# A two-layer encoder step on one core: the first feed-forward input projection in front of the memory projections

## The chip, the core and the metric

The kernel runs on one core of a Trainium2 chip. The metric is the device time of one execution in microseconds (us). A core has TensorE (PE: matmuls, transposes), VectorE (DVE), ScalarE (ACT), GpSimd (POOL) and SyncE (SP, which here only issues DMA transfers). Each engine runs its own program in order; they meet at semaphores alone.

## What is computed

One inference step of a two-layer encoder over R = 320 rows: 256 prompt rows and 64 sample rows, width 1024. Cut to what matters here:

```
def macaron_half(x, g, w_in, w_out):
    a, b = jnp.split(rms_norm(x, g) @ w_in, 2, axis=-1)
    return x + 0.5 * ((jax.nn.silu(a) * b) @ w_out)

def memory_kv(mem, g_mem, w_mkv, g_km):
    km, vm = jnp.split(rms_norm(mem, g_mem) @ w_mkv, 2, axis=-1)
    km = rms_norm(km.reshape(B, M, H_MEM, HEAD_DIM), g_km)
    return km, vm.reshape(B, M, H_MEM, HEAD_DIM)

```

`macaron_half` (width 1024 to 2 x 2816 and back) stands before and after the attention of each layer, four times in all; `memory_kv` is computed once for each layer from the 256 memory rows. Layer 0 has differential attention beside memory attention, layer 1 forgetting attention over keys and values shared from the stream, beside memory attention. The memory's keys and values of both layers are outputs too. They are needed first in the attention of layer 0.

## The kernel before

**Precision by splits.** Every weight and every stationary or moving operand of a projection is split into a rounded part `hi` and a remainder `lo`. A product is three matmuls (whi x xhi, whi x xlo, wlo x xhi; lines 434 to 436 in `product`), eight input tiles of 128 rows make one output tile, so a tile is 24 matmuls (66 in `out`, which has 22 input tiles).

**Stages.** The table `STAGES` gives the order: mkv0, mkv1 (the memory projections, 4 tiles of 256 columns each: 2 of keys, 2 of values), in0 (44 tiles of 320 columns: 11 blocks of 2 gate and 2 up tiles), out0 (8 tiles, 4 blocks of 2), pa, attention 0, wo0, in1, out1, kv, in2, out2, pb, attention 1, wo1, in3, out3. The stage's place in the table sets the counts on which all engines wait.

**Weights.** They stream through two slots: SyncE loads 1024 KB (in `out` 704 KB) into `raw[slot]` when `lo_ready[slot]` says the last content is split; ScalarE rounds it to `whi` (`split_hi`, line 821) once TensorE is done with the old one; VectorE subtracts to `wlo` (`split_lo`, line 1109). Slot 0 holds the first two tiles of a block, slot 1 the last two.

**Inputs.** ScalarE makes xhi times the norm's gain (`input_hi`, 858), VectorE xlo (`input_lo`, 1166). The norm's scale `r` comes later: ScalarE squares the eight tiles into two buffers `sq` (`stream_square`, 864, which waits for GpSimd's sum of two squares before), GpSimd sums them (`add_squares`, 1522 and 1525), TensorE spreads the sum by one matmul after the stage's first tile (`row_norm`, 444), ScalarE takes the root after a table load (829 to 838), VectorE a Newton step (1119 to 1125). VectorE multiplies each result by `r` as it leaves its bank (kmT, vT line 1185; gate 1203; up 1207). ScalarE's silu and hhi (898, 906), VectorE's hid and hlo (1210, 1214) make the hidden tile.

**Heads.** Keys get a norm of each head: squares (854; GpSimd 1535, 1540), `head_stat` on TensorE (459, 461), `head_root` on ScalarE and VectorE, then a tail, `tail_mkv`: TensorE transposes the values (488), VectorE copies them into vm (1160), TensorE broadcasts the root through the same two banks (478), VectorE scales kmT (1142).

**The order at the start.** SyncE loads the first weight half of mkv0 and the memory in four pieces each, in turn, then slot 1, mkv1, x, in0. GpSimd issues five table loads (`const_loads`, 1594) and then sums. ScalarE splits the pieces and then squares, TensorE starts on piece 1. mkv0 has `early_split=True`: ScalarE and VectorE split mkv1's slot 0 before mkv0's norm. The input of mkv1 is prepared in mixhi, mixlo during mkv0. The tail of mkv0 lies in in0's block 0 after its tile 1, that of mkv1 after the first tile of in0's block 2, while VectorE does it right after block 1:

```
            ffn_in("in0", left_mkv, lambda j: tail_mkv(1, "mkv1") if j == 0 else None)
```

In `ffn_out`, VectorE's block is: split of slot 0, x update (1240), xlo, split of slot 1, twice.

## Time and profile before

| | us |
|---|---|
| runs, device time | 1417.89, 1419.96, 1420.51 (median 1419.96) |
| profiled execution, its own time | 1417.31 |
| its span | 1415.2 |
| TensorE busy with matmuls | 1313.8 (93%) |
| VectorE busy | 769.6 (54%) |
| ScalarE busy | 568.3 (40%) |
| GpSimd busy | 184.8 (13%) |
| mean granted clock of TensorE | 0.967 of full speed |
| first matmul of in0 / out0 / pa | 52.25 / 213.72 / 292.47 |

The times of rows count from the span's start. A row of a timeline has the start, the length, and in brackets the engine's idle time before it with what ended it. Matmuls overlap in their pipeline, so the distance between starts tells their rate, not the length. The granted clock is given as a share of 2.4 GHz; 0.50 is the lower level, 1.2 GHz.

### The profile page before, as it was taken

The page shows a single profiled execution, that of the slowest core. Times are in us where ns is not written, and L with a number is a line of the kernel's source. Part 1 is how long each engine was busy: PE and PEld are TensorE (multiplying, and loading weights), DVE is VectorE, ACT ScalarE, POOL GpSimd, SP SyncE. Part 2 cuts the span into 40 slices and gives each one's busy share as a digit, 9 for nine tenths or more (in the row PEclk, how much of TensorE's full clock was granted, in tenths as well). Part 3 has the DMA queues.
Part 4 walks back from the last instruction along what each step waited for, and adds up shares of the span by engine and source line. Part 5 has one row for each costly group of instructions (what it writes and reads, how often), then busy time and mean ns, then how long its engine had stood idle before and what let it go on. Part 6 is the DMA issues. An engine that isn't in the chain of part 4 may idle for free.

```text
span 1415.2 us, 22134 instructions
## 1 busy us (share of the span) xinstructions
PE 1313.8 (93%) x8545; PEld 1271.6 (90%) x8545; DVE 769.6 (54%) x1230; ACT 568.3 (40%) x801; POOL 184.8 (13%) x201
## 2 busy tenths in 40 slices
PE   5799999999866999999999999999995789999999
PEld 5799999998754999999999989999983569999999
DVE  5665654455764565554455565654446545656533
ACT  6543333353343453333344433333343435333331
POOL 3400000054034100000022000001061231000000
PEclk9999999999988999999999999999996999999999
DMA  7544463443220144453444434444440004444343
GB/s 247 129 149 149 148 205 135 147 175 120 91 84 1 66 162 151 150 185 124 143 163 150 145 118 148 148 142 141 164 163 35 1 27 153 149 148 148 115 159 120
DMA packets 39065, 187.38 MB, mean 132 GB/s; under 512 B 4173, under 2 KB 14163, under 8 KB 23777
## 3 DMA queue, kind: packets, MB, share of 16 engines
q1 hardware_dynamic: 37824, 183.38, 37.9%
q0 software_dynamic: 1040, 3.13, 0.9%
q8 instruction: 38, 0.62, 0.2%
q10 hardware_dynamic: 144, 0.11, 0.1%
q14 instruction: 19, 0.15, 0.0%
HBM read 179.70 MB, written 6.90 MB: 132 GB/s over the span
## 4 chain that ended last, share of the span: by engine, by line
PE 81%; DVE 7%; ACT 5%; POOL 3%; issue 3%; DMA 1%; SPq 0%; ACTq 0%; DVEq 0%; POOLq 0%
PE bank L434 24%; PE bank L436 24%; PE bank L435 24%; ACT whi L821 2%; PE bank L689 1%; PE bank L690 1%; PE bank L691 1%; POOL ew L1569 1%; DVE wlo L1109 1%; PE bank L605 1%; PE bank L623 1%; DVE qz L1149 1%; ACT ew L972 1%; DVE ew L1288 1%; POOL ssum L1525 1%
## 5 line engine op out<-in xcount | busy, mean ns | idle before, releaser
L434 PE MATMUL bank<-xhi,whi 128*128 128x320 f32 (+1 forms) x1760 | 550.7, 313 | 22.1 <-DVE xlo L1166 11.3
L435 PE MATMUL bank<-xlo,whi 128*128 128x320 f32 (+1 forms) x1760 | 547.1, 311 | 0.0
L436 PE MATMUL bank<-xhi,wlo 128*128 128x320 f32 (+1 forms) x1760 | 546.9, 311 | 0.0
L1109 DVE TENSOR_TENSOR wlo<-raw,whi 128x2048 fp32r<-128x2048 f32 (+1 forms) x183 | 378.0, 2066 | 248.0 <-ACT whi L821 248.0
L821 ACT ACTIVATE whi<-raw 128x2048 fp32r<-128x2048 f32 (+1 forms) x183 | 315.4, 1723 | 244.4 <-PE bank L436 244.3
L434 PEld LDWEIGHTS bank<-xhi,whi 128*128 128x128 f32 x1760 | 334.2, 190 | 25.3 <-issue 14.8
L435 PEld LDWEIGHTS bank<-xlo,whi 128*128 128x128 f32 x1760 | 334.5, 190 | 0.5
L436 PEld LDWEIGHTS bank<-xhi,wlo 128*128 128x128 f32 x1760 | 334.3, 190 | 0.0
L434 PE MATMUL bank<-hhi,whi 128*128 128x320 f32 x704 | 219.5, 312 | 0.3 <-DVE wlo L1109 0.2
L436 PE MATMUL bank<-hhi,wlo 128*128 128x320 f32 x704 | 217.6, 309 | 0.0
L435 PE MATMUL bank<-hlo,whi 128*128 128x320 f32 x704 | 217.5, 309 | 0.0
L434 PEld LDWEIGHTS bank<-hhi,whi 128*128 128x128 f32 x704 | 132.1, 188 | 4.1 <-DVE wlo L1109 3.8
L435 PEld LDWEIGHTS bank<-hlo,whi 128*128 128x128 f32 x704 | 132.2, 188 | 0.0
L436 PEld LDWEIGHTS bank<-hhi,wlo 128*128 128x128 f32 x704 | 132.1, 188 | 0.0
L906 ACT ACTIVATE hhi<-hid 128x320 f32 (+1 forms) x88 | 40.8, 463 | 135.1 <-DVE hid L1210 135.1
L898 ACT ACTIVATE silu<-gate 128x320 f32<-128x320 f32 x88 | 40.8, 463 | 120.4 <-DVE gate L1203 120.4
L1203 DVE TENSOR_TENSOR gate<-bank,r 128x320 f32<-128x320 f32 x88 | 42.4, 487 | 81.3 <-PE bank L436 80.8
L1522 POOL COPY ssum<-sq 128x320 f32<-128x320 f32 (+1 forms) x7 | 6.1, 877 | 557.5 <-ACT sq L939 532.4
L1525 POOL TENSOR_TENSOR ssum<-ssum,sq 128x320 f32<-128x320 f32 (+1 forms) x49 | 46.3, 945 | 227.4 <-ACT sq L939 186.8
L623 PE MATMUL bank<-early,ew 128*128 128x128 f32 x136 | 24.5, 312 | 38.6 <-POOL ew L1569 31.1
L1214 DVE TENSOR_TENSOR hlo<-hid,hhi 128x320 f32 (+1 forms) x88 | 42.9, 488 | 31.2 <-ACT hhi L906 31.2
L1207 DVE TENSOR_TENSOR up<-bank,r 128x320 f32<-128x320 f32 x88 | 42.9, 487 | 26.7 <-PE bank L436 26.7
(205 smaller groups left out, 1156.2 us busy)
## 6 DMA issues: line engine op xcount, KB each, us to landing
raw<-in_w_ffn_in SPq DMA_DIRECT2D x88, 1024.0 KB, 4.8
raw<-in_w_ffn_out SPq DMA_DIRECT2D x64, 704.0 KB, 4.1
raw<-in_w_in_a SPq DMA_DIRECT2D x10, 1024.0 KB, 4.8
raw<-in_w_out SPq DMA_DIRECT2D x8, 1024.0 KB, 4.8
raw<-in_w_kv SPq DMA_DIRECT2D x6, 1024.0 KB, 4.7
raw<-in_w_in_b SPq DMA_DIRECT2D x4, 1024.0 KB, 4.8
raw<-in_w_mkv SPq DMA_DIRECT2D x3, 1024.0 KB, 4.8
x<-in_xT SPq DMA_DIRECT2D x1, 1280.0 KB, 9.4
```

The costliest lines, as they stand in the source:

```text
L434: mm(acc, wh, mhi(ks[q]), start=start and q == 0, stop=False)
L435: mm(acc, wh, mlo(ks[q]), start=False, stop=False)
L436: last = mm(acc, wl, mhi(ks[q]), start=False, stop=stop and q == nk - 1)
L623: last = nc.tensor.transpose(aux[b][:, to:to + P], ew[:, u % 2, at:at + P], ident[:])
L821: nc.scalar.activation(whi[slot][:, 0:size], raw[slot][:, 0:size], ACT.Copy).then_inc(hi_ready[slot], 1)
L898: nc.scalar.activation(silu[:, c, :], gate[:, c, :], ACT.Silu).then_inc(silu_out, 1)
L906: nc.scalar.activation(hhi[:, bass.ds(2 * i + c, 1), :], hid[:, c:c + 1, :], ACT.Copy).then_inc(hh_ready, 1)
L1109: tt(wlo[slot][:, 0:size], raw[slot][:, 0:size], f32(whi[slot][:, 0:size]), ALU.subtract).then_inc(lo_ready[slot], 1)
L1203: tt(gate[:, c, :], banks[c][:, 0:R], r[:], ALU.mult).then_inc(acc_free, 1)
L1207: tt(up[:, c, :], banks[2 + c][:, 0:R], r[:], ALU.mult).then_inc(acc_free, 1)
L1214: tt(hlo[:, bass.ds(2 * i + c, 1), :], hid[:, c:c + 1, :], f32(hhi[:, bass.ds(2 * i + c, 1), :]), ALU.subtract).then_inc(hl_ready, 1)
L1525: nc.gpsimd.tensor_tensor(ssum[:, 0:w], ssum[:, 0:w], sq[:, k % 2, 0:w], ALU.add).then_inc(ssum_step, 1)
```

## The change

in0 becomes the first stage, mkv0 and mkv1 stand between in0 and out0. x and in0's first half come in four pieces. GpSimd issues the table loads only after the last piece has landed. The memory is loaded behind the second pair of in0; mkv0's input is prepared in two buffers of its own (memhi, memlo) by `memory_in` after in0's blocks 0 to 2. That of mkv1 is written into xhi, xlo once in0 is done with them, during mkv0. `early_split` is gone from the projections; in0 has one split ahead of its norm's silu. The tails of both layers move into out0, after its blocks 0 and 1. The stores of the memory's outputs and the cache loads stand in front of out0's last pair. The order of buffers in memory changes with it (the values go to vmT).

```diff
-STAGES = [("mkv0", 1, 4, KD), ("mkv1", 1, 4, KD),
-          ("in0", 11, 44, KD), ("out0", 8, 8, 0), ("pa", 5, 20, KD), ("wo0", 2, 8, 0),
+STAGES = [("in0", 11, 44, KD), ("mkv0", 1, 4, KD), ("mkv1", 1, 4, KD), ("out0", 8, 8, 0), ("pa", 5, 20, KD), ("wo0", 2, 8, 0),
```

SyncE:

```diff
             for q in range(4):
-                sp.dma_start(raw[0][:, 512 * q:512 * (q + 1)], a["w_mkv"][0][:, 512 * q:512 * (q + 1)]
+                sp.dma_start(x[:, 2 * q:2 * q + 2], x_v[:, 2 * q:2 * q + 2]).then_inc(d_x[q], 16)
+                sp.dma_start(raw[0][:, 512 * q:512 * (q + 1)], weights["in0"][0][:, 512 * q:512 * (q + 1)]
                              ).then_inc(d_piece[q] if q < 3 else landed[0], 16)
-                sp.dma_start(memt[:, 2 * q:2 * q + 2], mem_v[:, 2 * q:2 * q + 2]).then_inc(d_mem[q], 16)
...
+            load_stage("in0", 1, 2)
+            sp.dma_start(memt[:], a["memT"].rearrange("(k p) r -> p k r", p=P)).then_inc(d_mem, 16)
+            load_stage("in0", 2)
+            load_stage("mkv0")
             load_stage("mkv1")
...
+            load_stage("out0", 0, 7)
...
-            load_stage("out0")
...
+            load_stage("out0", 7)
```

TensorE (`biases` is the relative bias matmul after the first block's last tile):

```diff
+            def left_mkv(i):
+                if i == 0:
                     head_stat("mkv1", 0, N_MEM)
                     head_stat("mkv1", 1, N_MEM)
+                    tail_mkv(0, "mkv0")
+                else:
+                    tail_mkv(1, "mkv1")
...
-            projection("mkv1", N_MEM, [], 4, xin=(mixhi, mixlo), after=stats_mkv0)
-            ffn_in("in0", left_mkv, lambda j: tail_mkv(1, "mkv1") if j == 0 else None)
-            ffn_out("out0")
+            ffn_in("in0", biases)
+            pe.wait_ge(bias_in, 1)
+            projection("mkv0", N_MEM, [], 4, xin=(memhi, memlo))
+            projection("mkv1", N_MEM, [], 4, after=stats_mkv0)
+            ffn_out("out0", left_mkv)
```

ScalarE:

```diff
             for q in range(4):
+                act.wait_ge(d_x[q], 16)
+                for k in (2 * q, 2 * q + 1):
+                    input_hi(x[:, k, :], xhi[:, k, :], "ffn1_0", k)
                 act.wait_ge(d_piece[q] if q < 3 else landed[0], 16)
...
                 for k in (2 * q, 2 * q + 1):
-                    input_hi(memt[:, k, :], xhi[:, k, 0:N_MEM], "mem0", k)
-            for k in range(4):
-                stream_square(0, k, memt[:, k, :], N_MEM)
+                    stream_square(NORM["in0"], k, x[:, k, :], R)
             split_hi(1, 0, BLK, None, 0)
...
+            def memory_in(i):
+                if i == 0:
+                    act.wait_ge(d_mem, 16)
+                    for k in range(KD):
+                        input_hi(memt[:, k, :], memhi[:, k, :], "mem0", k)
+                else:
+                    for k in range(4 * i - 4, 4 * i):
+                        stream_square(NORM["mkv0"], k, memt[:, k, :], N_MEM)
+
+            ffn_in("in0", memory_in)
+            act.wait_ge(acc_ready, TILE0["mkv0"])
             for k in range(KD):
-                input_hi(x[:, k, :], xhi[:, k, :], "ffn1_0", k)
+                input_hi(memt[:, k, :], xhi[:, k, 0:N_MEM], "mem1", k)
```

VectorE, `ffn_out` (after each of the first two blocks, `left_mkv` does the tail of one layer), and GpSimd:

```diff
+                if after:
+                    for i in range(2):
+                        body(i, None)
+                        after(i)
...
+            pool.wait_ge(landed[0], 16)
             for dst, src in const_loads:
                 pool.dma_start(dst[:], src).then_inc(d_const, 16)
```

What it moves, at three places. **ScalarE's start**, before: `whi<-raw 128x512` is a weight piece, `xhi` two tiles of the input, `sq` their squares; the brackets name the semaphores waited for.

```order
L858 ACTIVATE xhi<-memt,early 128x256 [waits d_mem1]
L858 ACTIVATE xhi<-memt,early 128x256
L1022 ACTIVATE whi<-raw 128x512 [waits d_piece2]
L858 ACTIVATE xhi<-memt,early 128x256 [waits d_mem2]
L858 ACTIVATE xhi<-memt,early 128x256
L1022 ACTIVATE whi<-raw 128x512 [waits landed0]
L858 ACTIVATE xhi<-memt,early 128x256 [waits d_mem3]
L858 ACTIVATE xhi<-memt,early 128x256
L864 ACTIVATE sq<-memt 128x256 x2
L864 ACTIVATE sq<-memt 128x256 [waits ssum_step] x2
L821 ACTIVATE whi<-raw 128x2048 [waits landed1]
L864 ACTIVATE sq<-memt 128x256 [waits ssum_step] x4
```

Now:

```order
L1040 ACTIVATE whi<-raw 128x512 [waits d_piece1]
L879 ACTIVATE sq<-x 128x320 [waits ssum_step] x2
L873 ACTIVATE xhi<-x,early 128x320 [waits d_x2]
L873 ACTIVATE xhi<-x,early 128x320
L1040 ACTIVATE whi<-raw 128x512 [waits d_piece2]
L879 ACTIVATE sq<-x 128x320 [waits ssum_step] x2
L873 ACTIVATE xhi<-x,early 128x320 [waits d_x3]
L873 ACTIVATE xhi<-x,early 128x320
L1040 ACTIVATE whi<-raw 128x512 [waits landed0]
L879 ACTIVATE sq<-x 128x320 [waits ssum_step] x2
L836 ACTIVATE whi<-raw 128x2048 [waits landed1]
```

The squares, which wait for GpSimd's sums (`ssum_step`), moved from behind the pieces to between them. In GpSimd's program, now:

```order
L1622 DMA select<-in_select 128x1309 [waits landed0]
L1622 DMA late<-in_late 128x281
L1622 DMA hot<-in_hot 32x384
L1622 DMA table<-in_table 32x6
L1622 DMA lamv<-in_lamv 128x256
L1548 COPY ssum<-sq 128x320 [waits sq_ready]
L1551 ISA
L1551 TENSOR_TENSOR ssum<-ssum,sq 128x320 [waits ssum_step,sq_ready] x7
```

Its first table load waits for the last weight piece (`landed0`); before it waited for nothing.

**ScalarE between the two memory projections**, before (from the second layer's input on):

```order
L858 ACTIVATE mixhi<-memt,early 128x256 x8
L821 ACTIVATE whi<-raw 128x2048 [waits acc_ready,landed0]
L838 ACT_TABLE_LOAD
L829 ACTIVATE rt<-outs,early 128x256 [waits ms_ready]
L831 ACTIVATE rt<-rt 128x256 [waits root]
L833 ACTIVATE rt<-rt 128x256 [waits root]
L854 ACTIVATE hsq_hi<-kmT 128x256 [waits acc_free] x2
L821 ACTIVATE whi<-raw 128x2048 [waits acc_ready,landed1]
```

Now (from the same input on):

```order
L873 ACTIVATE xhi<-memt,early 128x256 [waits acc_ready]
L873 ACTIVATE xhi<-memt,early 128x256 x7
L853 ACT_TABLE_LOAD
L844 ACTIVATE rt<-outs,early 128x256 [waits r_ready,ms_ready]
L846 ACTIVATE rt<-rt 128x256 [waits root]
L848 ACTIVATE rt<-rt 128x256 [waits root]
L869 ACTIVATE hsq_hi<-kmT 128x256 [waits acc_free]
L836 ACTIVATE whi<-raw 128x2048 [waits acc_ready,landed0]
L869 ACTIVATE hsq_hi<-kmT 128x256 [waits acc_free]
L836 ACTIVATE whi<-raw 128x2048 [waits acc_ready,landed1]
```

The split of mkv1's slot 0 (the first `whi<-raw 128x2048`) stood before the table load and the root, and stands behind them and behind the first key tile's square (`hsq_hi`).

**The tails**, TensorE before, the one of mkv1 behind the first tile of block 2 (`early,vT` are the transposes, `rs,select` the broadcast):

```order
L436 MATMUL bank<-xhi,wlo 128x320
L488 MATMUL bank<-early,vT 128x128 [waits aux_free,acc_free,bias_in]
L488 MATMUL bank<-early,vT 128x128
L488 MATMUL bank<-early,vT 128x128 [waits aux_free]
L488 MATMUL bank<-early,vT 128x128
L478 MATMUL bank<-rs,select 128x256 [waits aux_free,hr_ready]
L478 MATMUL bank<-rs,select 128x256 [waits aux_free]
```

TensorE now, the first tail, behind out0's block 0 (`early,vmT` the transposes):

```order
L444 MATMUL bank<-hhi,wlo 128x320
L467 MATMUL outs<-hsq_hi,select 128x256 [waits hsq_ready,hr_ready]
L469 MATMUL outs<-hsq_lo,select 128x256 [waits hlo_ready]
L467 MATMUL outs<-hsq_hi,select 128x256 [waits hsq_ready]
L469 MATMUL outs<-hsq_lo,select 128x256 [waits hlo_ready]
L496 MATMUL bank<-early,vmT 128x128 [waits acc_free]
L496 MATMUL bank<-early,vmT 128x128 x3
L486 MATMUL bank<-rs,select 128x256 [waits aux_free,hr_ready]
L486 MATMUL bank<-rs,select 128x256 [waits aux_free]
L442 MATMUL bank<-hhi,whi 128x320 [waits acc_free,lo_ready0]
```

and VectorE now, from the second tile of block 0 on:

```order
L1127 TENSOR_TENSOR wlo<-raw,whi 128x1408 [waits hi_ready0]
L1257 SCALAR_TENSOR_TENSOR x<-bank,x 128x320 [waits acc_ready]
L1261 SCALAR_TENSOR_TENSOR xlo<-x,early,xhi 128x320 [waits xn_hi]
L1127 TENSOR_TENSOR wlo<-raw,whi 128x1408 [waits hi_ready1]
L1178 COPY vm<-bank 128x256 [waits aux_ready,d_scratch]
L1178 COPY vm<-bank 128x256 [waits aux_ready]
```

The broadcast waits for `aux_free`, which VectorE's copy into vm gives, behind its split of 1408 columns. Before, the tails lay in in0, with VectorE's rows for the first ahead of block 0.

## Rows read from the trace of the kernel before

**Rows 1.** The page's span; DMA view: issues, KB each, us to landing.
```profile
span 1415.2 us, 22134 instructions
...
memt<-in_memT SPq DMA_DIRECT2D x4, 256.0 KB, 7.5
...
early<-in_early ACTq DMA_DIRECT2D x1, 105.5 KB, 3.7
```

**Rows 2.** Stretches: PE, PEld, DVE, ACT, POOL busy, granted clock, DMA share, GB/s.
```profile
4.00:6.00 2.00, 0.00 (x0) 0.00 (x0) 0.00 (x0) 1.32 (x2) 0.12 (x1) 1.00 1.07 381
52.00:54.00 2.00, 1.75 (x6) 1.75 (x7) 1.79 (x4) 2.00 (x2) 1.41 (x2) 0.50 0.56 72
54.00:56.00 2.00, 2.00 (x12) 2.00 (x11) 1.90 (x6) 1.39 (x2) 0.00 (x0) 0.71 0.96 298
```

**Rows 3.** Timeline of TensorE: start us, us, line, operation [idle before <- releaser].
```profile
7.86 0.55 PE L434 MATMUL bank<-xhi,whi 128*128 128x256 f32 x1 [7.86 <-DVE xlo L1166]
...
20.09 0.39 PE L434 MATMUL bank<-xhi,whi 128*128 128x256 f32 x1 [2.13 <-DVE wlo L1109]
...
39.17 0.28 PE L434 MATMUL bank<-mixhi,whi 128*128 128x256 f32 x1
...
44.80 0.28 PE L436 MATMUL bank<-mixhi,wlo 128*128 128x256 f32 x1
...
52.25 0.64 PE L434 MATMUL bank<-xhi,whi 128*128 128x320 f32 x1 [7.17 <-DVE wlo L1109]
...
89.87 0.62 PE L478 MATMUL bank<-rs,select 64*128 64x256 f32 x2 [1.28 <-DVE vm L1160]
...
90.42 0.41 PE L434 MATMUL bank<-xhi,whi 128*128 128x320 f32 x1
...
213.72 0.31 PE L434 MATMUL bank<-hhi,whi 128*128 128x320 f32 x1
...
292.47 0.31 PE L434 MATMUL bank<-xhi,whi 128*128 128x320 f32 x1
```

**Rows 4.** Timeline of ScalarE, same columns.
```profile
5.96 0.63 ACT L1022 ACTIVATE whi<-raw 128x512 fp32r<-128x512 f32 x1
...
21.86 3.29 ACT L858 ACTIVATE mixhi<-memt,early 128x256 fp32r<-128x256 f32 x8
...
25.05 1.90 ACT L821 ACTIVATE whi<-raw 128x2048 fp32r<-128x2048 f32 x1
...
26.98 1.28 ACT L838 ACT_TABLE_LOAD   x1
...
33.83 3.72 ACT L858 ACTIVATE xhi<-x,early 128x320 fp32r<-128x320 f32 x8
...
44.71 0.47 ACT L864 ACTIVATE sq<-x 128x320 f32<-128x320 f32 x1 [0.55 <-POOL ssum L1525]
```

**Rows 5.** Timeline of VectorE, same columns.
```profile
22.39 3.74 DVE L1166 SCALAR_TENSOR_TENSOR mixlo<-memt,early,mixhi 128x256 fp32r<-128x256 f32 x8 [2.35 <-ACT mixhi L858]
...
26.99 2.29 DVE L1109 TENSOR_TENSOR wlo<-raw,whi 128x2048 fp32r<-128x2048 f32 x1 [0.86 <-ACT whi L821]
...
29.67 0.42 DVE L1119 SCALAR_TENSOR_TENSOR rt<-outs,rt 128x256 f32<-128x256 f32 x1 [0.39 <-ACT rt L833]
...
30.92 0.76 DVE L1185 TENSOR_TENSOR kmT<-bank,r 128x256 f32<-128x256 f32 x2
...
226.69 1.63 DVE L1109 TENSOR_TENSOR wlo<-raw,whi 128x1408 fp32r<-128x1408 f32 x1 [0.92 <-ACT whi L821]
```

**Rows 6.** Timeline of GpSimd, same columns; first and last of five table loads, sums.
```profile
1.24 0.74 POOL L1594 DMA_DIRECT2D select<-in_select  x1 [0.80 <-POOLq L1738]
...
3.51 0.60 POOL L1594 DMA_DIRECT2D lamv<-in_lamv  x1
...
18.08 5.38 POOL L1525 TENSOR_TENSOR ssum<-ssum,sq 128x256 f32<-128x256 f32 x4 [0.86 <-ACT sq L864]
```

**Rows 7.** Timeline of SyncE: the eighth of the nine first transfers.
```profile
5.42 0.46 SPq L368 DMA_DIRECT2D memt<-in_memT  x1
```

More of the change, by code:

```diff
@@ L209, in encoder_kernel @@
         with ExitStack() as region:
+            memhi = sb("memhi", [P, KD, N_MEM], F32R, region)
+            memlo = sb("memlo", [P, KD, N_MEM], F32R, region)
+        with ExitStack() as region:
             bias8 = sb("bias8", [P, H_A, 256], F32, region)
@@ L498, in projection @@
                     pair, slot, col = j // 4, (j // 2) % 2, j % 2
-                    if col == 0 and not (j == 0 and stage == "mkv0"):
+                    if col == 0:
                         pe.wait_ge(lo_ready[slot], n0 + pair + 1)
@@ L525, in body @@
                         slot, col = j // 2, j % 2
-                        if col == 0:
+                        if col == 0 and not (first and j == 0 and stage == "in0"):
                             pe.wait_ge(lo_ready[slot], n0 + i + 1)
@@ L531, in each @@
                             def each(k):
+                                if stage == "in0" and k % 2 == 0:
+                                    pe.wait_ge(piece_lo, k // 2 + 1) if k < 6 else pe.wait_ge(lo_ready[0], 1)
                                 pe.wait_ge(xn_lo, x0 + k + 1)
@@ L886, in projection, with ffn_in @@
                         after(j)
-            def ffn_in(stage, after_first=None, tail=None):
+            def ffn_in(stage, after=None):
                 n0, t0 = PAIR0[stage], TILE0[stage]
@@ L898, in body @@
                         nc.scalar.activation(silu[:, c, :], gate[:, c, :], ACT.Silu).then_inc(silu_out, 1)
-                        if c == 0:
+                        if c == 0 and not (stage == "in0" and isinstance(i, int) and i == 0):
                             split_hi(0, n0 + i + 1, BLK if size is None else size, acc_ready, t0 + 4 * i + 2)
@@ L1192, in projection, with ffn_in @@
                         after(j)
-            def ffn_in(stage, after_first=None, tail=None):
+            def ffn_in(stage, after=None):
                 n0, t0 = PAIR0[stage], TILE0[stage]
@@ L1198, in ffn_in @@
                     row_norm(stage, R)
+                if stage == "in0":
+                    split_lo(0, n0 + 1, BLK)
                 def body(i, size):
@@ L1203, in body @@
                         tt(gate[:, c, :], banks[c][:, 0:R], r[:], ALU.mult).then_inc(acc_free, 1)
-                    split_lo(0, n0 + i + 1, size)
+                    if not (stage == "in0" and isinstance(i, int) and i == 0):
+                        split_lo(0, n0 + i + 1, size)
                     for c in range(2):
@@ L1405, in tail_mkv @@
+            ffn_in("in0", memory_in)
+            inputs_lo("mkv1", "mem1", lambda k: memt[:, k, :], N_MEM)
+            projection("mkv0", N_MEM, 2, 4, lambda j: kmT[:, 0, j, :], lambda v: vmT[:, v, :], {})
+            projection("mkv1", N_MEM, 2, 4, lambda j: kmT[:, 1, j, :], lambda v: vmT[:, 2 + v, :], {1: "mkv0"})
             def tail_mkv(layer, st):
```

179 lines of the change are left out of this document (83 added, 96 removed).

## The prediction

> **What bounds the kernel now.** I read the page first: the span is 1415.2 us and the profiled execution itself 1417.3 [rows 1]. TensorE is the bound: in its steady part one output tile of the feed-forward input (24 matmuls of 320 columns) takes (213.72 - 90.42) / 35 = 3.52 us with nothing between [rows 3]. So a change of order can win only where TensorE now stands still or runs at its lower clock. The timeline of TensorE shows where [rows 3]. The first matmul starts at 7.86; it stands 2.13 us before 20.09 and 7.17 before 52.25, both times for VectorE's half of a weight split; a memory layer's tile takes (44.80 - 39.17 + 0.12) / 2 = 2.88 us at full clock. Everything up to the first matmul of stage pa at 292.47 is what the change rearranges; after that only one ScalarE table load in in2 goes, under TensorE work (cost nothing; if ScalarE were late there it would be 1.28 us, [rows 4]). Pure work before 292.47 is 8 x 2.88 + 44 x 3.52 + the 78.75 of out0 = 256.7 us, so 35.8 are lost there. This is what can be saved, and the question is how much the new order loses.
>
> **The clock.** After the 7.17 us pause the granted clock is 0.50 from 52 to 54 and 0.71 from 54 to 56 [rows 2]: 1.0 + 0.58 us of full speed less, minus the quarter of a microsecond before 52.25, is 1.4 us lost. I take 1.4 after each pause longer than 2 us.
>
> **1. The start.** What used to be the memory's 1024 KB is the stream's 1280 KB, in pieces between the weight pieces. ScalarE now does per piece two xhi (3.72 / 8 = 0.47 each), a 512-column split (0.63 long, the next starts after 0.55) and two squares (0.45 each), 2.4 us in all, from 5.96 on [rows 4]. Before, the squares stood behind all four pieces. Now square 2 waits for GpSimd's first sum, and GpSimd first waits for the last weight piece and issues its five table loads (1.24 to 4.11, so 2.9 us [rows 6]). The last piece's issue is the eighth, at about 5.4 [rows 7]. Landing took between 3.7 us (early) and 7.5 us (memt) [rows 1], so it lands between 9.1 and 12.9. I take 10.2, nearer the first, because GpSimd's 1 MB of tables no longer shares the way: the 2.4 MB at the 381 GB/s of 4 to 6 us [rows 2] take 6.3 us from about 2 us on. Then: tables issued 13.1, first sum 13.7, squares 2 and 3 at 13.8 and 14.7 (a square per 1.0 us at that pace, [rows 4]), piece 3's xhi and split until 16.7, two squares 17.6, piece 4 until 19.1, VectorE's half 19.7, the last squares 20.0. TensorE ends its first tile at 21.2, and the norm's matmul, which needs all eight sums (21.3), at 21.9. The next three tiles: 3 x 3.52, half of the 1.4 clock (the rest falls in the last pieces; taken as 0.5) and 0.8 for the bias matmul (an estimate, six 128 x 128 matmuls of work): the first block ends at **33.8**. Slot 1's weights are there in time: whi 20.0 to 21.9, wlo to 24.1, wanted at 26.
>
> The Trainium skill ("DMA: Bandwidth & Descriptors", Anatomy of one DMA) gives a transfer about 2.0 us fixed beside its bytes. By that, an estimate, the last piece would land at 2 + 6.3 + 2.0 = 10.3, and the sum would be 0.1 us more.
>
> **2. The other ten blocks.** 40 x 3.52 = 140.9. The memory's preparation moves into blocks 0 to 2: eight memhi on ScalarE (3.29) and eight memlo on VectorE (3.74, [rows 4, 5]). Behind them VectorE's gate products come, then ScalarE's split (1.90) and VectorE's (2.29). From block end E: hlo done E + 4.9, memlo E + 8.7, gates E + 9.7, whi E + 11.9, wlo E + 14.2, while TensorE wants it at E + 14.1. So this cover has no slack. In the next block GpSimd's squares of the memory hold ScalarE alike. I take 0.5 us; bounds 0 (it just fits) and 2 x 1.7 if a GpSimd sum is late each time. in0 ends at T = 33.8 + 140.9 + 0.5 = **175.2**.
>
> **3. mkv0 to mkv1.** TensorE: 4 x 2.88 + 0.4 for the norm = T + 11.9. Both other engines first do the second layer's input: ScalarE after its last hhi (T + 2.6) eight xhi until T + 5.9, VectorE after its split and hlo (T + 4.9) eight xlo until T + 8.7. ScalarE's table load and roots take from 26.98 to 29.67, 2.7 us [rows 4, 5], so T + 8.6; r is ready 1.25 us after VectorE starts (29.67 to 30.92), T + 10.0; first key tile 10.4, its square 10.8, whi of mkv1's slot 0 12.7, wlo T + 15.0. The early split, which stood ahead of the norm, is gone. TensorE pauses **3.1 us** and loses **1.4** of clock: mkv1 runs from T + 15.0 to 15.0 + 11.5 + 0.5 (statistics) + 1.4 = T + 28.4. Then out0's first bank waits for VectorE's third tile of mkv1, which stands behind the head root of mkv0: second tile T + 22.2, statistics, square and split until 24.4, square, table and roots 27.3, VectorE's root about 2.0 and the copy T + 29.8. Another **1.4** us. out0 starts at T + 29.8 = **205.0**, against 213.72 now: 8.7 us won so far.
>
> **4. out0.** The tails of both memory layers moved here, to the end of blocks 0 and 1. TensorE transposes the values and its next matmul, the broadcast, needs VectorE's first copy. VectorE reaches this copy only after it has finished the block. Now one such tail costs 1.28 us of waiting at 89.87 [rows 3], because TensorE does it a tile (3.5 us) after the block's end. In out0 a tile takes 78.75 / 8 = 9.84, so tile 0 ends at 213.72 + 9.84 = 223.56 and VectorE's last split, behind it, at 226.69 + 1.63 = 228.32 [rows 5]: 4.8 us later. Copy (0.4) and broadcast to stream again (90.42 - 89.87, and 0.15 to answer) make 5.9 us per block end; of these 1.2 to 1.7 are work, the rest is a pause above 4 us, with the clock's 1.4 behind it. Two of them: 2 x 7.3 = **14.6**. out0 ends at 205.0 + 78.75 + 14.6 = 298.4.
>
> **5. SP's queue.** Ahead of the last pair of out0 now stand four stores and four cache loads, 2304 KB; at 381 GB/s [rows 2] that is 6.2 us, with a 704 KB half ahead and one behind, some 10 us against a tile of 9.84 and 1.9 us of slack. Bounds 0 and 3 us, taken as 1.0, nearer zero. pa starts at **299.4**.
>
> **The sum.** 299.4 - 292.5 = +6.9 us. On the profiled execution 1417.3 that gives 1424.2; on the median of the runs shown (1420.0, which is 2.7 above it) 1426.9. I predict **1426 us**. A measurement can tell 0.2%, 2.8 us, from no change.
>
> **Rivals.** (a) *The start runs at the data's pace.* If GpSimd's sums do not hold ScalarE, piece 4 is split at 13.7 instead of 19.7: 6.0 us less, +0.9, 1421. For it: without the squares a piece costs ScalarE only 1.5 us. Against: the wait for the last piece and the five issues stand ahead of the first sum in GpSimd's program. 0.15.
> (b) *The tails in out0 cost only their work*, the other side. If VectorE had the copy done before its split, each tail would cost 1.8 us and no clock: 2 x (7.3 - 1.8) = 11.0 less, -4.1, about 1416. It decides where the pause falls under some 2.7 us per tail. For it: one tail in in0 cost a wait of 1.28 only. Against: VectorE's program has the split in front of the copy. 0.09.
> (c) *VectorE and GpSimd fall behind in blocks 0 to 2.* Four sums of GpSimd took 5.38 us from 18.08 on, beside a VectorE split, so 1.35 each and not 1.0 [rows 6]. One sum stuck behind a 2.29 us split at the start, and one in each of the two blocks, give 3 x 2.3 = 6.9, less the 0.5 taken, and with both pauses short the clock stays: +13, 1433. 0.16. The Trainium skill ("SBUF — State Buffer", SBUF: two separate sides) says that VectorE with two SBUF inputs and GpSimd take one port pair in turn, each for a whole instruction. By that rule, a sum that meets the split would wait all of it; the trace agrees in the one case above.
> (d) My forecast: 0.58; the remaining 0.02 is that the order itself has no effect.
>
> **Range and chances.** The unknowns around the forecast: landing -1.1 / +2.7, clock down to -4.7 (no fall at all), blocks -0.5 / +2.9, SP's queue -1 / +2, median or lowest run 2.7. With (a) and most of (c) inside, 1418 to 1434. Faster (below 1417.1): (b) and a tail, 0.10. Same (1417.1 to 1422.8): (a) and some of (d) by a high clock, 0.18. Slower: 0.72.
>
> **What would show it.** TensorE's first tile done at 21, a block end at 34; ScalarE's third square of the stream released by GpSimd at about 14; mkv1's first matmul released by VectorE's split after 3 us; in out0 two waits of the broadcast on VectorE's vm copy above 4 us each, with a granted clock near 0.5 behind each. I am wrong if pa starts before 292, if the waits in out0 are near 1.3, or if in0 ends much after 176.

## The result and the profile after

| | before | after |
|---|---|---|
| device time, median | 1420.24 (4 runs) | 1437.16 (1435.70 to 1439.63, 4 runs) |
| profiled execution, span | 1415.2 | 1433.9 |
| its first matmul of pa | 292.47 | 307.47 |
| from there to the span's end | 1122.7 | 1126.4 |

The ratio is 1.0123, interval [1.0103, 1.0143]: 17 us slower. The direction was forecast, the size was not: the sum had +6.9 us, the prediction was 1426 us, and the time lies 3 us above the upper end of its range (1434).

TensorE's timeline of the changed kernel, the answer to [rows 3] (start us, length us, engine, line, operation, idle time before it and what ended it):

```profile
7.71 0.60 PE L442 MATMUL bank<-xhi,whi 128*128 128x320 f32 x1 [7.71 <-DVE wlo L1398]
...
19.21 0.64 PE L442 MATMUL bank<-xhi,whi 128*128 128x320 f32 x1 [7.44 <-DVE wlo L1398]
...
24.40 0.73 PE L452 MATMUL outs<-ssum,early 128*128 128x320 f32 x1
...
36.48 0.81 PE L712 MATMUL bank<-hot,table 32*6 32x384 f32 x2
...
83.49 0.41 PE L442 MATMUL bank<-xhi,whi 128*128 128x320 f32 x1 [3.77 <-DVE wlo L1127]
...
183.69 0.28 PE L442 MATMUL bank<-memhi,whi 128*128 128x256 f32 x1
...
198.44 0.39 PE L442 MATMUL bank<-xhi,whi 128*128 128x256 f32 x1 [2.66 <-DVE wlo L1127]
...
212.15 0.38 PE L442 MATMUL bank<-hhi,whi 128*128 128x320 f32 x1 [1.47 <-issue]
...
236.68 0.62 PE L486 MATMUL bank<-rs,select 64*128 64x256 f32 x2 [4.02 <-DVE vm L1178]
...
263.60 0.82 PE L486 MATMUL bank<-rs,select 64*128 64x256 f32 x2 [4.66 <-DVE vm L1178]
...
297.70 0.41 PE L442 MATMUL bank<-hhi,whi 128*128 128x320 f32 x1 [1.97 <-DVE wlo L1127]
...
307.47 0.31 PE L442 MATMUL bank<-xhi,whi 128*128 128x320 f32 x1
```

The first block ends 0.73 us after the bias matmul starts, at 37.21. Blocks are counted from 0, so "the ten blocks" are blocks 1 to 10, and the pause before 83.49 lies before block 4. Against the forecast's marks:

| stretch | forecast | measured | difference |
|---|---|---|---|
| start to the first block's end | 33.8 | 37.21 | +3.4 |
| ten blocks | 141.4 | 146.48 | +5.1 |
| mkv0's start to out0's | 29.8 | 28.46 | -1.3 |
| out0's start to pa's | 94.4 | 95.32 | +0.9 |
| pa's start to the end | as before | +3.7 | +3.7 |

The sum of the last column, 11.8, and the forecast +6.9 make the 18.7 us between the spans.

**The start.** The timelines of ScalarE, VectorE and GpSimd, same columns:

```profile
14.31 0.47 ACT L879 ACTIVATE sq<-x 128x320 f32<-128x320 f32 x1 [5.28 <-POOL ssum L1548]
15.31 0.47 ACT L879 ACTIVATE sq<-x 128x320 f32<-128x320 f32 x1 [0.54 <-POOL ssum L1551]
...
18.85 0.61 ACT L1040 ACTIVATE whi<-raw 128x512 fp32r<-128x512 f32 x1
```

```profile
5.95 1.01 DVE L1184 SCALAR_TENSOR_TENSOR xlo<-x,early,xhi 128x320 fp32r<-128x320 f32 x2 [4.67 <-ACT xhi L873]
6.92 0.69 DVE L1398 TENSOR_TENSOR wlo<-raw,whi 128x512 fp32r<-128x512 f32 x1
...
19.08 2.23 DVE L1184 SCALAR_TENSOR_TENSOR xlo<-x,early,xhi 128x320 fp32r<-128x320 f32 x2
21.24 1.35 DVE L1398 TENSOR_TENSOR wlo<-raw,whi 128x512 fp32r<-128x512 f32 x1
```

```profile
10.93 0.74 POOL L1622 DMA_DIRECT2D select<-in_select  x1 [10.49 <-DMA raw<-in_w_ffn_in]
...
14.43 7.60 POOL L1551 TENSOR_TENSOR ssum<-ssum,sq 128x320 f32<-128x320 f32 x7 [0.16 <-POOL ssum L1548]
```

GpSimd waits for the last piece (landed at 10.6; 10.2 was taken), issues five loads, and only then makes its first sum; ScalarE's third square stands 5.28 us for it. So far this is the forecast (13.8 for that square). But VectorE's pair of xlo takes 2.23 us beside GpSimd's sums where it took 1.01 without them, and the piece's split 1.35 instead of 0.69. The last piece is done at 22.6, not at 19.7.

**Block 4.** ScalarE waits for a block of weights, and TensorE for VectorE's half behind it. The stretches (PE, PEld, DVE, ACT, POOL busy, granted clock, DMA share, GB/s) and the DMA view of the changed kernel from 50 to 85 us and, behind it, of the kernel before from 35 to 60 us (issues, KB each, us to landing):

```profile
79.12 1.91 ACT L836 ACTIVATE whi<-raw 128x2048 fp32r<-128x2048 f32 x1 [6.13 <-DMA raw<-in_w_ffn_in]
```

```profile
76.00:78.00 2.00, 2.00 (x16) 2.00 (x15) 0.00 (x0) 0.00 (x0) 0.00 (x0) 1.00 0.24 102
...
84.00:86.00 2.00, 2.00 (x11) 2.00 (x10) 1.25 (x3) 1.49 (x2) 0.00 (x0) 0.57 0.70 184
```

```profile
bias_scratch<-trel POOLq DMA_DIRECT2D x1, 576.0 KB, 18.8
```

```profile
raw<-in_w_ffn_in SPq DMA_DIRECT2D x3, 1024.0 KB, 9.6
...
bias_scratch<-trel POOLq DMA_DIRECT2D x1, 576.0 KB, 19.3
```

GpSimd writes the table of relative positions (6 partitions, short rows) to DRAM. The write is issued at 57.05 and has landed at 75.9. The 1024 KB issued at 64.35 land 14.7 us later, at 79.0, while 4.8 is the median. In the stretch from 76 to 78 us the write is done, and what is left of the loads still keeps only 0.24 of the DMA engines' time busy. Before, the same write was issued at 37.91 and took 19.3 us. Only one block of weights was issued while it ran (at 52.38, landing in 9.6 us), and TensorE has no pause behind it: there it was hidden.

**out0.** VectorE at the first tail: the split of slot 1 stands in front of the copy, as forecast.

```profile
234.57 1.63 DVE L1127 TENSOR_TENSOR wlo<-raw,whi 128x1408 fp32r<-128x1408 f32 x1 [1.07 <-ACT whi L836]
236.12 0.75 DVE L1178 COPY vm<-bank 128x256 f32<-128x256 f32 x2
```

Near its end SyncE issues four stores from 281.52, then four cache loads, then at 287.36 the last pair's weights, while the DMA engines are full:

```profile
281.52 0.40 SPq L366 DMA_DIRECT2D o_mkT<-kmT  x1
...
287.36 3.58 SPq L351 DMA_DIRECT2D raw<-in_w_ffn_out  x2
```

```profile
290.00:292.00 2.00, 2.00 (x15) 1.91 (x14) 0.57 (x1) 0.00 (x0) 0.00 (x0) 1.00 1.08 408
```

### The profile page after: what moved, and what is told of

It reads as the page before. It is cut to its first block, busy times and chain, and to the rows that moved or that the text cites. A ratio compares the mean times of both kernels' runs of the same rounds, so it can differ in the third digit from the quotient of the medians.

```text
span 1433.9 us, 22025 instructions
## 1 busy us (share of the span) xinstructions
PE 1320.0 (92%) x8545; PEld 1276.9 (89%) x8545; DVE 771.5 (54%) x1230; ACT 565.5 (39%) x799; POOL 182.9 (13%) x201
## 4 chain that ended last, share of the span: by engine, by line
PE 78%; DVE 7%; issue 5%; ACT 4%; POOL 3%; DMA 2%; SPq 1%; ACTq 0%; POOLq 0%; DVEq 0%
PE bank L442 23%; PE bank L444 23%; PE bank L443 23%; ACT whi L836 2%; DVE wlo L1127 2%; DMA raw<-in_w_ffn_in 1%; PE bank L701 1%; PE bank L703 1%; PE bank L702 1%; POOL ew L1595 1%; PE bank L617 1%; PE bank L635 1%; DVE qz L1167 1%; ACT ew L987 1%; PE bank L486 1%
## 5 line engine op out<-in xcount | busy, mean ns | idle before, releaser
L635 PEld LDWEIGHTS bank<-early,ew 128*128 128x128 f32 x136 | 17.3, 156 | 44.3 <-POOL ew L1595 35.3
L1228 DVE TENSOR_TENSOR up<-bank,r 128x320 f32<-128x320 f32 x88 | 42.9, 488 | 24.5 <-PE bank L444 24.4
```

Of the source, the lines that this page charges most:

```text
L635: last = nc.tensor.transpose(aux[b][:, to:to + P], ew[:, u % 2, at:at + P], ident[:])
L1228: tt(up[:, c, :], banks[2 + c][:, 0:R], r[:], ALU.mult).then_inc(acc_free, 1)
```

## Experiments

All start from the changed kernel. Times are medians, beside before's on the same chip. The last five columns are read from the profiled execution: "pa" is where TensorE starts on it, "behind pa" the time from there to the span's end; none means under 1 us.

| kernel | time, us | ratio, interval | first block's end | out0 starts | wait before the last pair | pa | behind pa |
|---|---|---|---|---|---|---|---|
| changed | 1437.16 | 1.0123 [1.0103, 1.0143] | 37.21 | 212.15 | 1.97 | 307.47 | 1126.4 |
| tables at once | 1433.07 | 1.0092 [1.0075, 1.0109] | 33.45 | 208.90 | 3.44 | 307.79 | 1123.4 |
| squares behind | 1435.17 | 1.0111 [1.0094, 1.0128] | 35.45 | 211.05 | 2.58 | 309.04 | 1124.2 |
| start alone | 1439.19 | 1.0145 [1.0117, 1.0172] | 38.03 | 213.53 | 1.99 | 310.91 | 1124.8 |
| table in paced pieces | 1431.56 | 1.0080 [1.0057, 1.0102] | 38.91 | 208.29 | 2.82 | 306.02 | 1124.1 |
| table whole, late | 1439.87 | 1.0138 [1.0123, 1.0154] | 37.29 | 215.01 | 1.86 | 310.82 | 1123.1 |
| pieces at once | 1435.35 | 1.0114 [1.0097, 1.0131] | 37.34 | 211.78 | 1.65 | 307.54 | 1123.4 |
| tails later | 1426.51 | 1.0049 [1.0032, 1.0065] | 38.08 | 213.40 | 2.98 | 300.79 | 1124.3 |
| early split back | 1434.21 | 1.0097 [1.0074, 1.0120] | 37.19 | 209.85 | 2.37 | 307.24 | 1126.5 |
| loads before stores | 1429.52 | 1.0066 [1.0043, 1.0089] | 37.57 | 212.72 | none | 305.78 | 1121.8 |
| all, order of "start alone" | 1413.64 | 0.9958 [0.9945, 0.9971] | 39.10 | 206.55 | none | 289.20 | 1124.8 |
| all, squares between | 1408.93 | 0.9921 [0.9908, 0.9935] | 32.91 | 200.35 | none | 282.98 | 1122.6 |

The intervals of "tables at once", "squares behind", "early split back", "pieces at once", "table whole, late" and "start alone" overlap with that of the changed kernel: what these edits are worth in the whole time is not settled, and they are read by their marks in the profile. The marks vary too. Six kernels besides the changed one share its program up to the table's write, and their first block ends between 37.19 and 38.91 with the changed kernel's at 37.21; a difference under 2 us there says little.

### The start

```diff
-            pool.wait_ge(landed[0], 16)
             for dst, src in const_loads:
```

> GpSimd issues its five table loads at once, as in the kernel before, with nothing else changed. Theory A (GpSimd's wait for the last piece plus 2.9 us of issues holds ScalarE's third square, which stood until 14.3): that square starts at about 8.5, the last piece is split at about 14 to 15 and not 22.6, the first block of in0 ends at about 32 and not 37.2; 4 to 5 us less than the change, ratio to before about 1.009. Rival B (the start is bound by the data, and the tables now share the way): the last pieces land near 12 to 13 and the first block ends at 35 or later, 0 to 2 us less.

Without GpSimd's wait the first block ends 3.8 us earlier, clear of that spread: the wait held the start. The loads do share the way, as rival B has it: the last piece lands at 12.9 instead of 10.6, so the wait had bought 2.3 us there. VectorE stays slow beside the sums (2.23 and 1.35 us), so the last piece is done at 18.0 and not at theory A's 14 to 15. The time is 4.1 us less, theory A's 4 to 5, but not for its reason: in the profile nothing of the gain is left where pa starts (307.79 against 307.47), and the 3.0 us that the span is shorter behind it belong to the open point at the end of the next section.

The next kernel leaves GpSimd's wait and puts the squares behind the four pieces:

> ScalarE's eight squares stand behind the four pieces, as in the kernel before; GpSimd's wait stays. Theory A (the squares between the pieces hold them, and GpSimd's sums slow VectorE's piece operations): the last piece is split before 15 with VectorE's xlo pairs at 1.0 us and the 512-column subtraction at 0.7 (they took 2.2 and 1.35 beside the sums), but the norm's matmul still waits for the eighth sum at about 22, so the first block ends at about 34.5, 2 to 3 us less than the change. Rival B (the sums, not the pieces, set the whole start, and slot 1's split behind the squares comes late): the first block ends at 36 to 37, no gain.

VectorE is now as fast as alone (1.01 and 0.68 us per piece), which shows what had slowed it, and the last piece is done at 12.5. TensorE then stands 7.88 us for the last sum and does the norm's matmul at 21.62 instead of 24.40. Behind this pause its matmuls start at the slow distance for longer (13.8 us from there to the block's end, 12.8 in the changed kernel), so 1.8 us are left at the block's end, between the two theories and about the size of the spread named above.

The third takes both, with slot 1's split in the middle of the squares:

```diff
-                for k in (2 * q, 2 * q + 1):
-                    stream_square(NORM["in0"], k, x[:, k, :], R)
+            for k in range(4):
+                stream_square(NORM["in0"], k, x[:, k, :], R)
             split_hi(1, 0, BLK, None, 0)
+            for k in range(4, KD):
+                stream_square(NORM["in0"], k, x[:, k, :], R)
```

> Only the start differs from the changed kernel: GpSimd's table loads issued at once, and the second slot's split after the first four squares instead of after all eight. Theory A (the start's 3.4 us over the forecast are GpSimd's wait for the last piece, which holds up the squares, and with them the norm and the split of slot 1): the first block with the bias product ends at 32.5 to 33.5 instead of 37.21, the time is 4 us less, 1433. Theory B (VectorE slowed beside GpSimd's sums is what costs, and both orders run them side by side): the first block ends at 34.5 or later, 1435 or more.

Theory A missed: the block ends at 38.03, no earlier than in the changed kernel. Theory B's numbers hold, but it is not VectorE that is slowed (1.01 and 0.69 us at every piece). TensorE, and GpSimd's sums by line (count, then length min/median/max in ns):

```profile
24.27 1.43 PE L452 MATMUL outs<-ssum,early 128*128 128x320 f32 x2 [8.54 <-POOL ssum L1553]
```

```profile
L1553 POOL TENSOR_TENSOR ssum<-ssum,sq x7: 857/861/2608, 15.0 to 23.4; 128x320 f32<-128x320 f32 x7
```

The sums begin only at 14.2, behind the four pieces, and one took 2608 ns instead of 861: the one that began at 18.6 beside VectorE's 2048-column split (18.20 to 20.49). So the norm's matmul comes at 24.27, where it was at 24.40. That is what the prediction's rival (c) had named, found at the start and not in the blocks.

### The table of relative positions

Eight pieces of 72 KB, one block of in0 apart:

```diff
-            pool.dma_start(scratch.rearrange("p h x -> h p x"),
-                           trel[:].unsqueeze(1).broadcast_to([H_A, 64, NREL + 1])).then_inc(d_scratch, 16)
...
+            for q in range(8):
+                pool.wait_ge(acc_ready, 4 * (q + 3))
+                pool.dma_start(scratch.rearrange("p h x -> h p x")[:, 8 * q:8 * q + 8],
+                               trel[:].unsqueeze(1).broadcast_to([H_A, 8, NREL + 1])).then_inc(d_scratch, 16)
```

> The one 576 KB transfer of the bias table into its scratch is cut into eight of 72 KB, each issued by GpSimd one block of in0 apart, from block 2 on. Theory A (this transfer held the weight load issued at 64.35, which took 14.7 us instead of 4.8, and so TensorE for 3.8 us before 83.49 and some 1.3 of clock): no weight load in in0 takes over 8 us, no wait before block 4, in0 ends about 5 us earlier (178 to 179), ratio about 1.0085. Rival B (the load was late through SyncE's queue or the memory's 1 MB in front of it, whatever the scratch transfer does): the load stays near 14 us and the wait near 3.8.

No wait is left in the ten blocks, and no load there takes over 5.2 us; the blocks take 140.9 us, which is 40 tiles of 3.52: theory A. Then the whole transfer, but 65 us later:

> Only the write of the table of relative positions is moved: whole as in the changed kernel (one transfer of 576 KB), but started when the seventh block of the first projection is done (about 122 us) instead of at 57. Theory A (any 1 MB block of weights issued while that transfer runs lands some 10 us late, wherever it stands, and the buffers cover only part of that): the wait of 3.8 us before block 4 at 83.5 is gone, and one of 2 to 5 us stands between 135 and 160, ScalarE's wait for raw ahead of it; the time stays at 1436 to 1438. Theory B (only the crowd of early transfers, with the memory's own load and the first blocks catching up, made the wait): no wait over 1 us anywhere in the eleven blocks, and the time is 1432, as with the eight pieces.

Its timelines of TensorE and ScalarE have the wait where theory A put it:

```profile
147.46 0.63 PE L442 MATMUL bank<-xhi,whi 128*128 128x320 f32 x1 [4.30 <-DVE wlo L1127]
```

```profile
143.10 1.91 ACT L836 ACTIVATE whi<-raw 128x2048 fp32r<-128x2048 f32 x1 [8.11 <-DMA raw<-in_w_ffn_in]
```

The block of weights issued at 126.49 took 16.5 us, the write beside it 18.2. So it is the transfer, not the crowd at the start; the time itself came out 2 us above theory A's. And the eight pieces without pauses between them:

> The write of the table of relative positions is issued where the change has it (57 us), but as eight transfers of 72 KB one after the other, without a pause between them. The bytes and their time are the same, only the cut is another. Theory A (the whole transfer has only a few DMA engines, since the 0.24 to 0.32 of the engines' time at 74 to 80 us is nearly all its own; eight small ones are dealt out over more engines): all eight have landed within 12 us of the first issue instead of 18.8, the blocks of weights of that time land within 8 us, and the wait before block 4 falls under 1 us: 1432. Theory B (it is the 576 KB of short rows that cost, however they are cut): the last piece lands some 19 us after the first issue, the wait before block 4 stays at 3 to 4.5 us, and the time at 1436 to 1438.

Theory B for the transfers. The DMA engines' time is nearly full, at 33 GB/s where the share is 0.76 (stretches of this kernel, columns as above), and the last piece lands 14.7 us after its issue at 61.2: the whole takes 18.7 us, as in one transfer. Theory A leaned on shares of 0.24 to 0.32 at 74 to 80 us in the changed kernel as the write's own; but the write had landed at 75.9, and from 76 on they are the loads'. The wait before block 4 fell to 0.69 us, but the loads were not freed: the block of weights is issued at 68.16 instead of 64.35 and lands at 78.7, against 79.0 in the changed kernel.

```profile
60.00:64.00 4.00, 4.00 (x30) 4.00 (x29) 0.00 (x0) 1.35 (x4) 3.63 (x7) 1.00 1.06 95
64.00:68.00 4.00, 1.76 (x13) 1.50 (x11) 2.31 (x2) 2.01 (x2) 0.74 (x1) 1.00 0.76 33
```

TensorE comes to it later because of a pause that neither theory had: 2.36 us before 68.12. ScalarE's and GpSimd's timelines give its chain: the eight issues stand ahead of the memory's first sum in GpSimd's program, and ScalarE's square, and the silu and the split behind it, wait for that sum.

```profile
62.18 0.42 ACT L879 ACTIVATE sq<-memt 128x256 f32<-128x256 f32 x1 [7.52 <-POOL ssum L1548]
```

```profile
57.18 4.57 POOL L1626 DMA_DIRECT2D bias_scratch<-trel  x8 [35.24 <-DVE trel L1410]
```

Block 4 starts at 83.15 instead of 83.49. The ten blocks take 144.5 us, between 140.9 and 146.5; most of the 2.0 us won is the clock, which reads 0.57 behind block 4's pause in the changed kernel and 1.00 here. Of these three ways only the paced pieces, behind the sums, cost nothing.

### The tails in out0

TensorE gets each tail half a tile later, between the two halves of the next block's first tile:

```diff
-                    after(0)
-                    body(1, False)
-                    after(1)
+                    body(1, False, lambda: after(0))
+                    body(2, False, lambda: after(1))
```

> TensorE does the two tails in out0 half a tile later (behind the first 33 matmuls of the next block) and VectorE's program stays. Theory A (TensorE stood 4.0 and 4.7 us for VectorE's copy behind its split, and then ran at the lower clock): each wait falls under 1 us, no clock loss behind it, out0 is 9 to 11 us shorter (95.3 now), ratio about 1.005. Rival B (the copy itself or the answer between the engines is slow, or ScalarE's head root for mkv1 holds VectorE): the waits move along with the tails and stay above 3 us.

The largest single gain, 10.7 us, and theory A, though out0 became 7.9 us shorter and not 9 to 11. Its two tails on TensorE wait 0.46 and 0.39 us instead of 4.02 and 4.66, and out0 takes 87.4 us instead of 95.3. The rest went at the last pair: its pause grew from 1.97 to 2.98 us, and from there to pa TensorE took 11.3 us instead of 9.8, at the lower clock. Of the 10.7 us, 2.1 lie behind pa, where the program is unchanged.

### Between mkv0 and mkv1, and the queue

> The change dropped the rule that, in mkv0, the split of slot 0 for the next stage goes ahead of the squares and the leaving of the tiles. This kernel puts the rule back on ScalarE and VectorE; nothing else differs from the changed kernel. Theory A (the pause between mkv0 and mkv1, 2.66 us ended by VectorE's weight split, is caused by the order on the two engines): the pause falls under 1 us, the clock of the tiles behind it comes back (1.4), out0 starts at 208 to 209.5 instead of 212.15, the whole is 3 to 4 us less, about 1433.5. Theory B (the pause stands for the raw block's landing or for the slot still being read, which no order changes): the pause stays at 2 to 3 us and the time at 1436 to 1438.

The edit is `early_split=True` on mkv0, on ScalarE and VectorE. The pause falls from 2.66 to 0.75 us and out0 starts 2.3 us earlier, nearly as theory A says. There was no clock to come back: it had stayed at 1.00 behind the pause (below). The wait before the last pair grows, and pa starts only 0.2 earlier. The time is 3.0 us less, with intervals that overlap: the pause is explained, what it is worth alone is not settled.

```diff
-            load_stage("out0", 0, 7)
+            load_stage("out0")
+            load_stage("pa", 0, 1)
...
-            load_stage("out0", 7)
-            load_stage("pa")
+            load_stage("pa", 1)
```

> Only the order on SP's queue differs from the changed kernel: the last block of out0 and the first pair of pa are issued ahead of the stores of the memory's keys and values, the caches behind pa. Theory A (the 1.97 us wait before out0's last pair, and ScalarE's 5.62 us wait for raw ahead of it, stand for loads issued late behind the stores and caches): that wait goes, pa starts 2 to 3.5 us earlier (304 to 305.5 instead of 307.47), the whole is about 1434.5. Theory B (the raw buffers come free too late, or the loads are slow in landing, whatever stands ahead of them): the wait stays within 0.5 us of 1.97 and the time at 1436 to 1438.

The cache loads now stand behind pa. The wait is gone and pa starts 1.7 us earlier, a little less than theory A said. The time fell by 7.6, where theory A had some 2.7, and of that 4.3 lie between the starts of pa and wo0, which no wait explains (below).

### All together

The first of these has the squares' order of "start alone":

> All mendings at once on the changed kernel: GpSimd's table loads issued at once, the second slot's split after four squares, the table of relative positions written to DRAM in eight pieces one block apart, the two tails half a tile later, mkv0's early split back, the loads ahead of the stores. Theory A (the places are separate and their costs add up): 1437 less 4 (start), 5 (block 4's wait), 10 (tails), 3.5 (mkv0 to mkv1), 2 (queue), about 1412 and thus 7 under the kernel before, pa starting at about 283. Theory B (the places share a cover, so that what is won at one is lost at the next, or the clock takes part of it): less than two thirds of it, 1420 or more, no faster than the kernel before.

1413.6, close to theory A's 1412, and 6.6 us under before. But pa starts at 289.2 and not at 283: the start of "start alone" is in it, and the first block ends at 39.10. And with the squares where the change put them:

> As the kernel with all mendings, but the squares stay where the change put them, two behind each piece, instead of four behind the last piece and four behind the split of slot 1. Theory A (the first block ends by the last of GpSimd's sums: the squares between the pieces let the sums begin early, and the split of slot 1 between the squares slows GpSimd's sums): the first block with the bias product ends at 33.5 instead of 39.1, pa starts at 283.5 instead of 289.2, the time is 5 to 6 us less than 1413.6, about 1408, ratio to before 0.992. Theory B (later stages are paced by something fed from the queue, so an earlier start is only waited away): first block at 33.5, but the time within 2 us of 1413.6.

TensorE's timeline in this kernel:

```profile
32.91 0.41 PE L442 MATMUL bank<-xhi,whi 128*128 128x320 f32 x1
...
173.81 0.28 PE L442 MATMUL bank<-memhi,whi 128*128 128x256 f32 x1
...
186.65 0.35 PE L442 MATMUL bank<-xhi,whi 128*128 128x256 f32 x1 [0.76 <-issue]
...
200.35 0.38 PE L442 MATMUL bank<-hhi,whi 128*128 128x320 f32 x1 [1.49 <-issue]
...
226.17 0.62 PE L486 MATMUL bank<-rs,select 64*128 64x256 f32 x2 [0.46 <-DVE vm L1179]
...
248.28 0.62 PE L486 MATMUL bank<-rs,select 64*128 64x256 f32 x2 [0.39 <-DVE vm L1179]
...
282.98 0.31 PE L442 MATMUL bank<-xhi,whi 128*128 128x320 f32 x1
```

Theory A again: 1408.9 us, 28.2 less than the changed kernel and 0.8% faster than the kernel before. pa starts 9.5 us before its old place [rows 3], and the two spans differ by 9.6 (1405.6 against 1415.2). Up to pa it is 24.5 us faster than the changed kernel: 4.3 at the start, 5.6 in the ten blocks, 1.9 from mkv0 to out0, 12.7 in out0. The order of the change is worth having; the places that were to cover its waits did not.

## Why the prediction was right in sign and wrong in size

The step that failed most is step 2: it put 0.5 us of waiting on the ten blocks, and they were 5.6 over their pure work, because of a transfer that the step left out. Two smaller ones failed with it: step 1 put 0.6 us on VectorE's half of the last piece, which was 3.1, and nothing was put down behind pa, where the profile has 3.7 us more. The time lies 3.2 us above the range, so with step 2 or the part behind pa right it would have been inside. The tails, the largest term, were right.

**Step 1, the start: mechanism right, one term missing.** GpSimd's wait held ScalarE as forecast, and the squares came within 0.6 us of their marks. Missing was VectorE's slowing by GpSimd's sums: the step took VectorE's half of piece 4 as 0.6 us after ScalarE's, and it was 3.1 (22.6 against 19.5). This made the norm 2.5 us late (24.40 against 21.9); the rest, 0.9, is the lower clock going on behind it: the matmuls after 24.40 start 0.267 us apart until about 26.2, 0.147 later. The prediction held the port rule of the Trainium skill ("SBUF — State Buffer", SBUF: two separate sides) against GpSimd alone. The two orders of squares show it both ways: VectorE's pair of xlo 2.23 us instead of 1.01 beside sums, a sum 2.6 instead of 0.86 beside a split. The lengths fit the rule, by which the one that comes second waits until the other's instruction is done. The last piece's landing was estimated with the Trainium skill's 2.0 us fixed for a transfer ("DMA: Bandwidth & Descriptors", Anatomy of one DMA) at 10.3, and it was 10.6; that section gives the figure for transfers that GpSimd issues, and SyncE issued these.

**Step 2, the ten blocks: right on what it looked at, wrong in what it left out.** The cover in blocks 0 to 2, without slack by the working, held with no wait at all (0.5 was taken): in block 1 VectorE's split ended 12.3 us after the block's start (49.5 against 37.2), where 14.2 was forecast and 14.1 was wanted. The 5.6 us over 140.9 came from a transfer that the prediction does not name, though the diff shows GpSimd's program around it. It was hidden before, when nothing waited for the one block of weights beside it, so no row on waits pointed at it. The pause was 3.77, and the granted clock reads 0.57 and 0.58 in the two stretches of 2 us from 84 us on. Rival (c), the sums and splits falling behind each other in these blocks, has the time nearest to the measured one (1433); its number came near for another reason, as no pause stands in blocks 1 to 3. Its price of 1.35 us for each of four sums [rows 6] is a mean of one of 2.54 and three of 0.73 to 0.94: one sum met the split, as in "start alone".

**Step 3: the pauses right, the clock not.** The pause was forecast at 3.1 and was 2.66; out0's first bank cost 1.47 against 1.4. Bringing the early split back removed most of the first. But the 1.4 us of clock added behind the pause did not come. The stretch from 200 to 204 us in the changed kernel and, behind it, in "table whole, late" (columns as above):

```profile
200.00:204.00 4.00, 4.00 (x36) 4.00 (x35) 1.68 (x2) 0.00 (x0) 0.61 (x1) 1.00 0.79 253
```

```profile
200.00:204.00 4.00, 4.00 (x22) 4.00 (x22) 2.61 (x3) 0.00 (x0) 0.34 (x1) 0.57 0.62 193
```

The pause ahead of it is 2.66 us in both. From mkv0's start to out0's the first takes 28.46 us and the second 29.96. So the price of 1.4 was about right where the clock falls; that it falls behind every pause over 2 us, as the prediction took it, was not. Here this error worked against the others: the stretch came out 1.3 us short.

**Step 4: right.** Waits of 4.02 and 4.66 us, above 4 each, released by VectorE's copy behind its split; out0 took 95.3 us. The granted clock behind them reads 0.73 from 236 to 240 and 0.50 from 264 to 268. The edit that removes only the two waits gives back 7.9 us in out0, and 2.5 more that the last pair took again; the forecast for both tails was 14.6, of which 2 x 1.2 to 1.7 are work that stays. Rival (b) is ruled out.

**Step 5: right in kind, low in size.** 1.0 was taken and 1.97 came, inside its bounds. What the step did not see is that this queue takes back part of what is won ahead of it: with the queue's order kept, the five kernels that came to the last pair earlier (by 0.6 to 9.2 us) waited longer there (3.44, 2.58, 2.82, 2.98, 2.37 against 1.97), the three that came later 1.65 to 1.99. That is not all of it. In "tables at once" out0 starts 3.3 us earlier and pa 0.3 later: of these 3.6 us, 1.5 are the longer wait, 1.5 the lower clock behind it (from the pause to pa 11.3 us instead of 9.8) and 0.6 lie between the two tails. "Start alone" has 11.3 us there too, behind a wait of 1.99. With the queue mended, the two last kernels are 6.2 us apart at out0's start and still 6.2 at pa.

**Behind pa**, costed at nothing, the profile has 3.7 us more. There the program is the same; this part took 1122.7 us before, 1126.4 after, and in the eleven kernels of the experiments 1121.8 to 1126.5, without order in their edits. All of the difference lies before wo0: from wo0's start on all thirteen take 951.0 to 951.5 us. TensorE's idle times between pa and wo0 add up to 32.5 to 35.1 us and do not order the kernels either ("loads before stores", the fastest there, has 35.1, the changed one 33.1). The granted clock does. It is read from 40 to 200 us behind pa's start:

| granted clock | kernels | behind pa, us |
|---|---|---|
| 0.86 | early split back | 1126.5 |
| 0.87 | changed | 1126.4 |
| 0.88 | tails later, start alone, all (order of "start alone") | 1124.3 to 1124.8 |
| 0.89 | before, squares behind, table in paced pieces | 1122.7 to 1124.2 |
| 0.90 | tables at once, table whole late, pieces at once, all (squares between) | 1122.6 to 1123.4 |
| 0.91 | loads before stores | 1121.8 |

The lines of the changed kernel and of the one before:

```profile
347.00:507.00 160.00, 127.18 (x674) 109.08 (x674) 91.27 (x257) 56.71 (x136) 38.39 (x48) 0.87 0.18 60
```

```profile
332.00:492.00 160.00, 127.82 (x698) 110.43 (x698) 93.12 (x259) 58.84 (x138) 39.25 (x49) 0.89 0.19 65
```

Why the clock falls more often there in one kernel than in another stays open. The changed kernel stands near the slow end, so each single gain but that of "early split back" has 1.6 to 4.6 us of this in its profile. The two kernels with all mendings gain 18.3 and 24.5 us up to pa, where this plays no part.

## What to carry to other kernels

When a stage moves, list all that is in flight at its new place, on every queue, and not only what the stage issues: a transfer that no wait names in the old trace can be the one that waits in the new. An operation that answers TensorE belongs ahead of the next weight split on its engine, or what asks for it belongs half a tile later. And before counting a small gain, look for the next queue that absorbs it; mend that one first. Where kernels differ by 2 or 3 us, compare the stretches in which their programs are the same: here these alone differed by up to 4.7 us.

## What the runs showed of the hardware

- One write of 576 KB in short rows from 6 partitions took 18.2 to 19.3 us and delayed a 1024 KB load issued while it ran from 4.8 to 14.7 us (16.5 in "table whole, late"). In these two kernels the load landed 3.1 and 2.5 us after the write had, and in the changed kernel the DMA engines' share was 0.24 in between. Cut into eight back to back the write took as long, at shares of 0.76 to 1.06, and a load issued 3.8 us later than the changed kernel's landed at the same moment (78.7 against 79.0). Eight pieces one block apart landed in 3.6 us each (median) and cost nothing.
- VectorE and GpSimd hold each other up in both directions, and the wait stands inside the length of the one that waits: 1.01 to 2.23 us for two operations, 0.86 to 2.6 for one.
- The same pause of TensorE can be followed by a fall of the granted clock or not: 2.66 us, then 1.00 in one kernel and 0.57 in another.
- At the very start the granted clock reads 1.00 between 24 and 26 us while matmuls of 320 columns start 0.267 us apart, the distance that they also have at 84 to 86 us, where the clock reads 0.57; the distance of starts tells the clock there, the column doesn't. The trace's first record of the clock begins at 26.2.
